# FFN down projection: the plain block moved from last to first, and the low parts of the other down weights made on VectorE instead of GpSimd

## The chip, the cores and the metric

The kernel runs on one core of a Trainium2 chip. The metric is the device time of one execution in microseconds (us); the times shown are medians of several runs.

## The reference

Two blocks on 1024 tokens of width 1024: first an RG-LRU with latent attention layer and an SSD layer, then a second block with gated convolution, stick-breaking attention, a feed-forward part and a gated per-layer embedding. The change concerns the end of the second block:

```
m = rmsnorm(h, g_mlp[i])
h = h + jnp.square(jax.nn.relu(m @ w_up[i])) @ w_down[i]
gate = jax.nn.sigmoid(rmsnorm(h, g_ple[i]) @ w_ple_gate[i])
h = h + gate * (p[i] @ w_ple_proj[i])
return rmsnorm(h, g_final)
```

`w_up` is 1024 x 4096 and `w_down` is 4096 x 1024.

## The kernel before

**Number format.** TensorE multiplies float32 values of reduced precision. Each operand is split into a high part and a low part (the value minus its high part), and each product is three matmuls: weight high with activation high, weight high with activation low, weight low with activation high. The high part of a weight is made by ScalarE (`down_hi`) or GpSimd (`plain_slab`), the low part by GpSimd (`down_part` at L946, `plain_slab` at L920). The parts live in `w_hi` and `w_lo`, a ring of eight entries of 128x256; an entry comes free when TensorE has finished the product that read it.

**Seven products.** The up and down projections are mostly computed as a two by two block product with seven instead of eight products (`SEVEN = [1, 6, 5, 7, 2, 3, 4]`). That needs sums and differences of weight quarters (`weight_sums`, four instructions of 128x256 on VectorE, L3448 to L3453) and of activations (`diff`, L3416, in `ffn_whole_u`). VectorE adds each product from PSUM into `H` or into `ffn_shared`, the part that three quadrants of the result have in common (`down_added`, L3477 and L3479). After all blocks `shared_added` (L3489) adds `ffn_shared` to the three quadrants of `H`.

**Order of work.** The hidden width 4096 is eight blocks of 512 (`FFN_BLOCKS`). The up projection runs over 16 pairs of slabs and stores its squared results to DRAM (`f_kept`). The down projection takes a block at a time, with the 512 x 1024 weights of a block in four slabs; a slab is seven products of six matmuls. Blocks 0 to 6 are done with seven products, block 7 (`last_down`, L1742) plainly, with 48 matmuls a slab. Then the gate's eight slabs follow (L991, `N_PLE`), which need the finished `H` in high and low parts (`raw_hi` on ScalarE, `raw_lo` on VectorE) and its squares (`raw_square`, `raw_add`).

**Queues.** Each engine works through an order written out by hand. On VectorE, a slab of the down projection is: wait for product i, add it; after the first add the four weight sums of the next slab; after some adds one step for the u tiles of the next block (`next_u_steps`: four differences in the second slab, four low parts in the third, three in the fourth, none in the first; L3416 and L3422). On ScalarE it is the seven high parts of the next slab (L2482), with the high parts of the next block's u (L2439) between them. GpSimd only makes low parts of weights there. SP issues all loads and stores: the next block's u tiles when the block before it is done, and each weight slab when the slab that held its place has been split.

**Waits of a product.** Product i on TensorE (`down`, L1720) waits for its weight's low part. In the first slab of a block it also waits for the low part of u. The fifth, sixth and seventh product of a slab share a PSUM bank with the first, third and fourth, and wait until VectorE has added those (`BEFORE = {2: 1, 3: 5, 4: 7}`); the first four wait for adds of the slab two earlier. The up pairs have the same scheme; the sixth product of the last pair waits for `c22` (L3367). In the last pair's VectorE order, two differences and a low part of block 0's u (`diff(5, 0)`, `u_lo(1, 0)`, `diff(6, 0)`) stand ahead of `u3` and `c22`.

Of the kernel before, what the change touches and what calls it, by code (L numbers as in the profile page):

```python
# [197 lines left out]
FFN_ORDER += [("down", _b, _s) for _b in range(DOWN_BLOCKS) for _s in range(4)]  # L198
FFN_ORDER += [("last", FFN_BLOCKS - 1, _s) for _s in range(4)]
# [27 lines left out]
for _n in range(pair_slab(PAIRS), N_PLE - 4):  # L227
    _uses(_n, 7, {6: _n + 1}, 1)
LAST_FREED = _freed
USED += USED[-1:] * (-len(USED) % RING)  # L230
for _n in range(N_PLE - 4, NSLAB):
    ENTRY[_n] = len(USED)
    USED += [("slab", _n + 1)] * 4
assert all(ENTRY[_n] % 4 == 0 for _n in range(N_PLE - 4, NSLAB))
DOWN_ADDS = 28 * DOWN_BLOCKS
# [18 lines left out]
HIGHS = [(_j, _b) for _b in range(FFN_BLOCKS) for _j in ((1, 5, 6, 7, 2, 3, 4) if _b < DOWN_BLOCKS else (1, 8, 2, 3))]  # L254
LOWS = [(_j, _b) for _b in range(FFN_BLOCKS) for _j in (SEVEN if _b < DOWN_BLOCKS else (1, 8, 2, 3))]
DIFFS = [(_j, _b) for _b in range(DOWN_BLOCKS) for _j in (5, 6, 7, 4)]
# [40 lines left out]
def product_turn(b, s, j):  # L297
    return 7 * (4 * b + s) + SEVEN.index(j) + 1
# [23 lines left out]
def program(nc, x_t, pos, w, vec, rows, consts, p_t, out):  # L322
    ctx = ExitStack()
    with ctx:
# [146 lines left out]
        def head_square_at(k):  # L471
# [25 lines left out]
        u_even_at = {1: raw_at, 4: raw_at + 8 * kb, 5: xh_at + 48 * kb, 3: xh_at + 56 * kb, 6: xh_at, 2: xh_at + 8 * kb, 7: xh_at + 16 * kb}  # L497
        u_odd_at = {1: raw_at + 16 * kb, 6: raw_at + 24 * kb, 5: raw_at + 32 * kb, 7: raw_at + 40 * kb,
                    2: xh_at + 32 * kb, 3: xh_at + 40 * kb, 4: xh_at + 24 * kb}
        u_plain_at = {8: xh_at + 24 * kb, 1: xh_at + 32 * kb, 2: xh_at + 40 * kb, 3: xh_at + 48 * kb}  # L500
        u_at = {"even": u_even_at, "odd": u_odd_at, "plain": u_plain_at, "later": {5: raw_at + 48 * kb}}
        U_SPLIT = {(name, j): place(at_, f"ffn_u_{name}{j}", [P, 2, 2, HB], F32R)[0] for name, table in u_at.items() for j, at_ in table.items()}
        U_WHOLE = {(name, j): place(at_, f"ffn_whole_u_{name}{j}", [P, 2, 2, HB], F32)[0] for name, table in u_at.items() for j, at_ in table.items()}
        PJ = (place(xh_at, "ple_proj_a", [P, 6, TOK], F32)[0], place(xh_at + 56 * kb, "ple_proj_b", [P, 2, TOK], F32)[0])
# [21 lines left out]
        def u_name(b, j):  # L526
            if b == DOWN_BLOCKS:
                return "plain", j
            if b % 2:
                return "odd", j  # L530
            return "later" if j == 5 and b else "even", j
# [105 lines left out]
        s_hk = sem("h_kept_then_ffn_plain_u_loaded")  # L637
# [41 lines left out]
        s_u7 = Part(s_hk, 16 * KT)  # L679
# [59 lines left out]
        def _(sp):  # L739
# [38 lines left out]
            def load(b, j):  # L778
                t, half = 0 if j in (1, 8) else 1, 0 if j in (1, 2) else HB
                to = 4 if j == 8 and b < DOWN_BLOCKS else j  # L780
                done = s_u7 if b == DOWN_BLOCKS else s_ur[b % 2][RAW_QUAD[j]]
                sp.dma_start(u_whole(b, to),
                             f_kept[2 * b:2 * b + 2, t, :, half:half + HB].rearrange("q p t -> p q t")).then_inc(done.sem, 16)

            d0 = pair_slab(PAIRS)
# [11 lines left out]
            next_slab(d0)  # L797
            next_slab(d0 + 1)
# [6 lines left out]
            used(pair_use(p, 1))  # L805
            load(0, 3)
            used(pair_use(p, 2))
            load(0, 2)
            store(p, 0)
            store(p, 1)  # L810
            for b in range(DOWN_BLOCKS):
                if b == 0:
                    used(pair_use(p, 6))
                    stored(4)
                else:
                    sp.wait_ge(s_slab, FFN_AT["down", b - 1, 3] + 1)
                    stored(2 * b + 4)
                for j in (1, 8, 3, 2):
                    load(b + 1, j)
                for s in range(2, 6):  # L820
                    next_slab(d0 + 4 * b + s)
            for n in range(d0 + 4 * DOWN_BLOCKS + 2, NSLAB):
# [12 lines left out]
        def _(pool):  # L835
# [112 lines left out]
            d0 = pair_slab(PAIRS)
# [21 lines left out]
        class Down:  # L970


            def wait(self, eng, k):
                eng.wait_ge(s_dr, DOWN_ADDS + k + 1)

        @block.tensor
        def _(pe):
# [747 lines left out]
            def last_down(q):  # L1725
# [2042 lines left out]
```

## Time and profile before

| | us |
|---|---|
| median of 3 runs | 2628.53 |
| lowest, highest | 2624.53, 2628.74 |
| the profiled execution | 2624.4 |
| its span | 2622.5 |
| TensorE busy | 2542.3 (97%) |
| VectorE busy | 1730.9 (66%) |
| ScalarE busy | 1147.0 (44%) |
| GpSimd busy | 1136.2 (43%) |

Busy times are of the profiled execution, whose own time is 2624.4 us. In the profile PE is TensorE, PEld its weight loads, DVE VectorE, ACT ScalarE, POOL GpSimd and SP SyncE. A busy time is a union over instructions, whose recorded durations overlap: from the start of one instruction to the start of the next is less than the duration.

### The profile page before, as it was taken

The page shows a single profiled execution, that of the slowest core. Times are in us where ns is not written, and L with a number is a line of the kernel's source. Part 1 is how long each engine was busy: PE and PEld are TensorE (multiplying, and loading weights), DVE is VectorE, ACT ScalarE, POOL GpSimd, SP SyncE. Part 2 cuts the span into 40 slices and gives each one's busy share as a digit, 9 for nine tenths or more (in the row PEclk, how much of TensorE's full clock was granted, in tenths as well). Part 3 has the DMA queues.
Part 4 walks back from the last instruction along what each step waited for, and adds up shares of the span by engine and source line. Part 5 has one row for each costly group of instructions (what it writes and reads, how often), then busy time and mean ns, then how long its engine had stood idle before and what let it go on. Part 6 is the DMA issues. An engine that isn't in the chain of part 4 may idle for free.

```text
span 2622.5 us, 33254 instructions
## 1 busy us (share of the span) xinstructions
PE 2542.3 (97%) x12712; PEld 2022.7 (77%) x12712; DVE 1730.9 (66%) x2061; ACT 1147.0 (44%) x1757; POOL 1136.2 (43%) x1100
## 2 busy tenths in 40 slices
PE   8999999999999999999999999999999998999997
PEld 7877888687787787887676777767888887878886
DVE  7636763677748648658776455565556668999856
ACT  3527882336405305316275545463333334444232
POOL 4633344532342432432441222214645556777652
PEclk9999999999999999999999999999999999999999
DMA  3111002212212112111230001002133333322412
GB/s 140 49 44 33 25 25 86 92 47 101 65 49 81 57 48 73 64 49 61 84 129 25 33 25 33 25 25 97 49 126 107 113 113 121 121 98 104 161 41 81
DMA packets 58137, 189.93 MB, mean 72 GB/s; under 512 B 5952, under 2 KB 6336, under 8 KB 57984
## 3 DMA queue, kind: packets, MB, share of 16 engines
q1 hardware_dynamic: 44704, 143.67, 16.1%
q10 hardware_dynamic: 13280, 44.17, 4.7%
q8 instruction: 102, 1.67, 0.3%
q14 instruction: 51, 0.42, 0.1%
HBM read 158.33 MB, written 29.49 MB: 72 GB/s over the span
## 4 chain that ended last, share of the span: by engine, by line
PE 80%; DVE 11%; ACT 5%; issue 3%; POOL 1%; ACTq 0%; DMA 0%; DVEq 0%; POOLq 0%; SPq 0%
PE PS L991 38%; PE PS L1697 10%; PE PS L1720 8%; PE PS L1321 4%; PE PS L1228 3%; PE PS L1742 2%; PE PS L1554 1%; PE PS L1537 1%; PE PS L1354 1%; PE PS L1127 1%; PE PS L1364 1%; PE PS L1358 1%; PE PS L1141 1%; PE PS L1577 1%; PE PS L1670 1%
## 5 line engine op out<-in xcount | busy, mean ns | idle before, releaser
L839 POOL CAST w_hi<-w_stage 128x1024 fp32r<-128x1024 f32 x130 | 144.4, 1111 | 1046.9 <-PE PS L991 756.9
L842 POOL TENSOR_TENSOR w_lo<-w_stage,w_hi 128x256 fp32r<-128x256 f32 x520 | 494.0, 981 | 10.4
L991 PE MATMUL PS<-XH,w_hi 128*128 128x512 f32 x1216 | 386.6, 399 | 9.0 <-ACT ssd_z L2136 3.3
L991 PE MATMUL PS<-XL,w_hi 128*128 128x512 f32 x1216 | 375.5, 390 | 0.0
L991 PE MATMUL PS<-XH,w_lo 128*128 128x512 f32 x1216 | 375.0, 390 | 0.0
L991 PEld LDWEIGHTS PS<-XH,w_hi 128*128 128x128 f32 x1216 | 221.4, 188 | 65.5 <-issue 12.9
L991 PEld LDWEIGHTS PS<-XL,w_hi 128*128 128x128 f32 x1216 | 228.2, 188 | 48.8
L991 PEld LDWEIGHTS PS<-XH,w_lo 128*128 128x128 f32 x1216 | 228.2, 188 | 48.6
L946 POOL TENSOR_TENSOR w_lo<-w_sums,w_hi 128x256 fp32r<-128x256 f32 x112 | 126.1, 1138 | 59.7 <-ACT w_hi L2482 59.1
L1697 PE MATMUL PS<-ffn_token_sums,w_hi 128*128 128x512 f32 x448 | 138.0, 389 | 0.0
L1720 PE MATMUL PS<-ffn_u_even,w_hi 128*128 128x512 f32 x400 | 125.6, 395 | 5.3 <-DVE ffn_shared L3477 3.2
L934 POOL TENSOR_TENSOR w_lo<-up_w_sums,w_hi 128x512 fp32r<-128x512 f32 x56 | 82.7, 1478 | 80.7 <-ACT w_hi L2470 80.5
L2096 ACT ACTIVATE ssd_x<-ssd_conv 128x1024 f32<-128x1024 f32 x16 | 16.9, 1060 | 227.2 <-DVE ssd_conv L2924 222.5
L1697 PE MATMUL PS<-ffn_raw,w_hi 128*128 128x512 f32 x336 | 104.7, 393 | 2.3 <-DVE ffn_t L3367 2.3
L1720 PE MATMUL PS<-ffn_u_odd,w_hi 128*128 128x512 f32 x336 | 104.3, 392 | 1.1 <-DVE H L3479 0.4
L3479 DVE TENSOR_TENSOR H<-H,PS 128x512 f32<-128x512 f32 x140 | 93.4, 679 | 17.0 <-PE PS L1720 15.5
L1697 PEld LDWEIGHTS PS<-ffn_token_sums,w_hi 128*128 128x128 f32 x448 | 84.1, 188 | 17.4
L1720 PEld LDWEIGHTS PS<-ffn_u_even,w_hi 128*128 128x128 f32 x400 | 74.8, 190 | 25.4 <-issue 7.7
L2924 DVE SCALAR_TENSOR_TENSOR ssd_conv<-PS,VC,ssd_conv 128x1023 f32<-128x1023 f32 (+2 forms) x72 | 92.3, 1282 | 2.6
L2922 DVE TENSOR_SCALAR ssd_conv<-PS,VC 128x1024 f32<-128x1024 f32 x24 | 32.2, 1343 | 92.6 <-PE PS L991 92.5
L3240 DVE TENSOR_TENSOR sb_z<-sb_z,PS 128x1024 f32<-128x1024 f32 (+3 forms) x48 | 45.8, 954 | 67.3 <-PE PS L1554 67.0
L946 POOL TENSOR_TENSOR w_lo<-w_stage,w_hi 128x256 fp32r<-128x256 f32 x84 | 82.5, 990 | 15.3 <-ACT w_hi L2482 15.3
(492 smaller groups left out, 6105.1 us busy)
## 6 DMA issues: line engine op xcount, KB each, us to landing
w_stage<-w SPq DMA_DIRECT2D x202, 512.0 KB, 3.3
ssd_sum_rows<-sums_kept ACTq DMA_DIRECT2D x32, 512.0 KB, 3.8
f_kept<-ffn_t SPq DMA_DIRECT2D x32, 512.0 KB, 2.6
ffn_whole_u_even<-f_kept SPq DMA_DIRECT2D x16, 512.0 KB, 4.8
ffn_whole_u_odd<-f_kept SPq DMA_DIRECT2D x12, 512.0 KB, 5.4
H<-x_t ACTq DMA_DIRECT2D x8, 512.0 KB, 8.2
pj_kept<-ple_proj_tiles ACTq DMA_DIRECT2D x8, 512.0 KB, 2.6
h_kept<-H ACTq DMA_DIRECT2D x8, 512.0 KB, 3.6
```

Source lines behind the costliest of these rows:

```text
L839: nc.gpsimd.tensor_copy(w_hi[:, slot, :, :], w_stage[:, slot, :, :]).then_inc(s_w_hi, 1)
L842: nc.gpsimd.tensor_tensor(w_lo[:, slot, k:k + 2, :], w_stage[:, slot, k:k + 2, :], w_hi[:, slot, k:k + 2, :].bitcast(F32), ALU.subtract).t ...
L934: nc.gpsimd.tensor_tensor(ring(w_lo, e, 2), src, ring(w_hi, e, 2).bitcast(F32), ALU.subtract).then_inc(done, count)
L946: nc.gpsimd.tensor_tensor(ring(w_lo, e), src, ring(w_hi, e).bitcast(F32), ALU.subtract).then_inc(done, count)
L991: mm = nc.tensor.matmul(outs[:, half, :], wt[:, slot, k, :], a[:, k - first, half * HB:(half + 1) * HB], start=(k == whole[0] and wt is w_ ...
L1228: mm = nc.tensor.matmul(PS[:, 2 * (n % 2) + half, :], wt[:, n % 2, k, :], a[:, k, half_cols(half)], start=(k == 0 and wt is w_hi and a is ...
L1321: mm = nc.tensor.matmul(PS[:, half, :], wt[:, n % 2, k, :], a[:, k, half * HB:(half + 1) * HB], start=(k == 0 and wt is w_hi and a is XH), ...
L1697: mm = nc.tensor.matmul(PS[:, 4 * (p % 2) + BANK[j], :], ring(wt, e + 2 * i + k // 2, k % 2), up_acts(j, hl, k), start=(j not in BEFORE an ...
L1720: mm = nc.tensor.matmul(PS[:, 4 * (d % 2) + BANK[j], :], ring(wt, e + i, k), down_acts(b, j, k, hl), start=(j not in BEFORE and k == 0 and ...
L1742: mm = nc.tensor.matmul(PS[:, 4 * (q % 2) + 2 * e + half, :], ring(wt, e0 + k // 2, k % 2), down_acts(DOWN_BLOCKS, quad, t % 2, hl), start ...
L2924: ins = v.scalar_tensor_tensor(out=y[:, d:TOK], in0=src[:, 0:TOK - d], scalar=wcol(3 - d), in1=y[:, d:TOK], op0=ALU.mult, op1=ALU.add)
L3479: v.tensor_tensor(dst, dst, src, ALU.add).then_inc(s_dr, 1)
```

## The change

- The plain block is block 0 and comes first (`plain_down`); blocks 1 to 7 follow with seven products. The numbers of matmuls stay the same.
- VectorE makes the low parts of the weights of the 28 slabs with seven products (`down_lo`), seven a slab, one ahead of each add. GpSimd keeps the plain slabs.
- The last pair's VectorE order has `u_lo(1, 0)` and `u_lo(8, 0)` ahead of `u3`, and `u_lo(2, 0)`, `u_lo(3, 0)` behind it. Differences and low parts of block 1's u are made beside the plain block.
- The shared sums are added inside the last block, after the second add of each slab. `last_tile` (raw_lo and the square's add) also stands inside the last block, and so do ScalarE's `gate_acts`.
- The u tiles have other places in memory. The loads of `pj_kept` are issued by SP instead of ScalarE.

```diff
-FFN_ORDER += [("down", _b, _s) for _b in range(DOWN_BLOCKS) for _s in range(4)]
-FFN_ORDER += [("last", FFN_BLOCKS - 1, _s) for _s in range(4)]
+FFN_ORDER += [("plain", 0, _s) for _s in range(4)]
+FFN_ORDER += [("down", _b, _s) for _b in range(1, FFN_BLOCKS) for _s in range(4)]
...
-            for d in range(4 * DOWN_BLOCKS):
-                for i in range(7):
-                    down_part(d, i)
-            for turn, n in enumerate(range(N_PLE - 4, NSLAB)):
-                plain_slab(n, 2 * PLAIN_PAIRS + turn)
+            for c in range(4):
+                plain_slab(PLAIN_DOWN + c, 2 * PLAIN_PAIRS + c)
+            pool.wait_ge(s_w_ready, 4 * N_PLE)
+            for c, n in enumerate(range(N_PLE, NSLAB)):
+                plain_slab(n, 2 * PLAIN_PAIRS + 4 + c)
...
+            def gate_acts(k):
                 Down().wait(act, k)
                 raw_hi(ple, "g_ple", k)
                 raw_square(ple, k)
+
+            for d in range(4 * DOWN_BLOCKS):
+                b = d // 4 + 1
+                highs = [j for j, b_ in HIGHS if b_ == b + 1]
+                for i in range(7):
+                    down_hi(d, i)
+                    if highs and d % 4 == 2 and i in (1, 3, 5):
+                        u_hi(highs[i // 2], b + 1)
+                    if highs and d % 4 == 3 and i in (1, 2, 4, 6):
+                        u_hi(highs[(1, 2, 4, 6).index(i) + 3], b + 1)
+                    if not highs and d % 4 and i == 5:
+                        gate_acts(2 * (d % 4 - 1))
+                    if not highs and d % 4 > 1 and i == 1:
+                        gate_acts(2 * (d % 4 - 1) - 1)
+            for k in range(5, KT):
+                gate_acts(k)
...
+            def down_lo(d, i):
+                n, j = SEVEN_DOWN + d, SEVEN[i]
+                e = ENTRY[n] + i
+                src = stage(n)[:, RAW_AT[j]:RAW_AT[j] + 2, :] if j in RAW_AT else WS[:, SUM_AT[j], :, :]
+                s_ah.wait(dve, 7 * (PAIRS - PLAIN_PAIRS) + 7 * d + i + 1)
+                done, count = (s_wd, 1) if i < 6 else (s_w_ready, 4)
+                v.tensor_tensor(ring(w_lo, e), src, ring(w_hi, e).bitcast(F32), ALU.subtract).then_inc(done, count)
...
+            def shared_added(s):
+                dve.wait_ge(s_dr, product_turn(FFN_BLOCKS - 1, s, 6))
+                for h in (H[:, 2 * s + 1, HB:TOK], H[:, 2 * s, HB:TOK], H[:, 2 * s + 1, 0:HB]):
+                    v.tensor_tensor(h, h, SHARED[:, s, :], ALU.add).then_inc(s_dv.sem, 1)
+
+            def down_added(b, s):
...
                 for i, j in enumerate(SEVEN):
+                    if ahead:
+                        down_lo(d + 1, i)
+                        if i == 0:
+                            weight_sums(*ahead)
...
+                    if end and i == 1:
+                        shared_added(s)
+                    if end and s and i == 2:
+                        last_tile(2 * s - 1)
+                    if end and i == 6:
+                        if s == 2:
+                            for slot in range(2):
+                                v.memset(SM[:, 4 + slot, 0:1], 0.0).then_inc(s_evac[slot], 4 * FFN_BLOCKS)
+                        last_tile(2 * s)
```

## Rows read from the trace of the kernel before

**Rows 1.** The page: busy line of the engines, and the chain's shares by engine.
```profile
PE 2542.3 (97%) x12712; PEld 2022.7 (77%) x12712; DVE 1730.9 (66%) x2061; ACT 1147.0 (44%) x1757; POOL 1136.2 (43%) x1100
...
PE 80%; DVE 11%; ACT 5%; issue 3%; POOL 1%; ACTq 0%; DMA 0%; DVEq 0%; POOLq 0%; SPq 0%
```
**Rows 2.** Windows: us, then busy (x) of PE, PEld, DVE, ACT, POOL; clock, DMA, GB/s.
```profile
2191.70:2274.40 82.70, 77.34 (x326) 61.01 (x324) 77.38 (x114) 38.15 (x75) 59.58 (x56) 0.98 0.33 115
...
2313.50:2352.90 39.40, 39.06 (x168) 31.21 (x169) 36.55 (x56) 17.19 (x36) 29.73 (x29) 1.00 0.32 108
2352.90:2392.00 39.10, 38.86 (x168) 31.27 (x168) 36.28 (x55) 17.23 (x36) 29.71 (x29) 1.00 0.30 108
```
**Rows 3.** The chain that ended last: start, us, what; end of the down projection.
```profile
2431.19 41.06 PE PS L1720 x180
2472.26 43.52 PE PS L1742 x192
```
**Rows 4.** Timelines of TensorE and VectorE, 2178 to 2204: start, us, instruction, idle before.
```profile
2184.53 0.70 PE L1697 MATMUL PS<-ffn_raw,w_hi 128*128 128x512 f32 x2 [2.31 <-DVE ffn_t L3367]
...
2196.13 0.70 PE L1720 MATMUL PS<-ffn_u_even,w_hi 128*128 128x512 f32 x2 [0.85 <-DVE ffn_u_even L3422]
2196.67 0.39 PE L1720 MATMUL PS<-ffn_u_even,w_lo 128*128 128x512 f32 x1
...
2202.35 1.19 PE L1720 MATMUL PS<-ffn_u_even,w_hi 128*128 128x512 f32 x2 [3.25 <-DVE ffn_shared L3477]
2203.34 0.63 PE L1720 MATMUL PS<-ffn_u_even,w_lo 128*128 128x512 f32 x1
...
2178.56 2.21 DVE L3422 TENSOR_TENSOR ffn_u_even<-ffn_whole_u_even,ffn_u_even 128x1024 fp32r<-128x1024 f32 x1
2180.69 2.31 DVE L3416 TENSOR_TENSOR ffn_whole_u_even<-ffn_whole_u_even,ffn_whole_u_even 128x1024 f32<-128x1024 f32 x1
```
**Rows 5.** Timeline of VectorE in one slab with four steps.
```profile
2338.54 0.46 DVE L3448 TENSOR_TENSOR w_sums<-w_stage 128x256 f32<-128x256 f32 x1
...
2339.37 0.42 DVE L3451 TENSOR_TENSOR w_sums<-w_stage 128x256 f32<-128x256 f32 x1
2339.71 0.42 DVE L3453 TENSOR_TENSOR w_sums<-w_stage,w_sums 128x256 f32<-128x256 f32 x1
2340.05 0.68 DVE L3479 TENSOR_TENSOR ffn_shared<-ffn_shared,PS 128x512 f32<-128x512 f32 x1
2340.64 1.23 DVE L3422 TENSOR_TENSOR ffn_u_even<-ffn_whole_u_even,ffn_u_even 128x1024 fp32r<-128x1024 f32 x1
2341.79 0.67 DVE L3479 TENSOR_TENSOR H<-H,PS 128x512 f32<-128x512 f32 x1
...
2348.83 0.46 DVE L3448 TENSOR_TENSOR w_sums<-w_stage 128x256 f32<-128x256 f32 x1
```
**Rows 6.** Groups of instructions, 2274 to 2430: busy us, mean ns, then idle before.
```profile
L946 POOL TENSOR_TENSOR w_lo<-w_sums,w_hi 128x256 fp32r<-128x256 f32 x65 | 75.1, 1167 | 31.2 <-ACT w_hi L2482 30.8
...
L2482 ACT ACTIVATE w_hi<-w_sums 128x256 fp32r<-128x256 f32 x64 | 24.3, 409 | 57.2 <-DVE w_sums L3450 49.3 <-PE PS L1720 7.5
...
L3422 DVE TENSOR_TENSOR ffn_u_even<-ffn_whole_u_even,ffn_u_even 128x1024 fp32r<-128x1024 f32 x12 | 15.8, 1316 | 0.0
```
**Rows 7.** Groups of VectorE, ScalarE (2472 to 2530) and GpSimd (2472 to 2600).
```profile
L3276 DVE SCALAR_TENSOR_TENSOR raw_lo<-H,VC,raw_hi 128x1024 fp32r<-128x1024 f32 x8 | 11.5, 1439 | 0.0
L3489 DVE TENSOR_TENSOR H<-H,ffn_shared 128x512 f32<-128x512 f32 x12 | 8.4, 770 | 0.0
...
L2394 ACT ACTIVATE raw_hi<-H,VC 128x1024 fp32r<-128x1024 f32 x8 | 9.2, 1151 | 39.3 <-DVE H L3495 30.6 <-DVE H L3499 8.7
L2403 ACT ACTIVATE ffn_t<-H 128x1024 f32<-128x1024 f32 x8 | 8.4, 1046 | 1.2 <-DVE square_sum L3285 1.2
...
L920 POOL TENSOR_TENSOR w_lo<-w_stage,w_hi 128x256 fp32r<-128x256 f32 x43 | 42.3, 995 | 0.0
L909 POOL CAST w_hi<-w_stage 128x256 fp32r<-128x256 f32 x42 | 25.8, 629 | 52.0 <-PE PS L991 29.1 <-PE PS L1742 22.9
```

More of the change, by code:

```diff
@@ L526, in u_name, with u_loaded @@
         def u_name(b, j):
-            if b == DOWN_BLOCKS:
+            if b == 0:
                 return "plain", j
-            if b % 2:
-                return "odd", j
-            return "later" if j == 5 and b else "even", j
+            if b == 1 and j == 4:
+                return "first", j
+            return ("even", "odd")[b % 2], j
+        def u_loaded(b):
+            return 16 * (b // 2 + 1)
         def down_acts(b, j, i, hl):
@@ L805, in _ @@
             used(pair_use(p, 1))
+            load(0, 2)
             load(0, 3)
-            used(pair_use(p, 2))
-            load(0, 2)
             store(p, 0)
@@ L2434, in u_hi @@
                 if j in RAW_QUAD:
-                    done, count = (s_u7, 64) if b == DOWN_BLOCKS else (s_ur[b % 2][RAW_QUAD[j]], 16 * (b // 2 + 1))
-                    done.wait(act, count)
+                    s_ur[b % 2][RAW_QUAD[j]].wait(act, u_loaded(b))
                 else:
@@ L3462, in next_u_steps @@
                 return {1: (u_lo, 2), 3: (u_lo, 3), 5: (u_lo, 4)}
-            def down_added(b, s, ahead, steps):
-                n, d = FFN_AT["down", b, s], 4 * b + s
+            def shared_added(s):
[3 more added lines that the diff above has]
+            def down_added(b, s):
+                n, d, end = FFN_AT["down", b, s], 4 * (b - 1) + s, b == FFN_BLOCKS - 1
+                ahead = None if end and s == 3 else (b, s + 1) if s < 3 else (b + 1, 0)
+                steps = next_u_steps(b + 1, s) if s and not end else {}
                 into = {1: SHARED[:, s, :], 6: SHARED[:, s, :], 5: H[:, 2 * s + 1, HB:TOK], 7: H[:, 2 * s + 1, HB:TOK],
@@ L3475, in down_added @@
                         dve.wait_ge(s_dr, product_turn(b, s, 1 if j == 6 else 5))
-                    if j == 1 and b == 0:
+                    if end and j in (5, 3, 4):
+                        s_dv.wait(dve, 3 * s + {5: 1, 3: 2, 4: 3}[j])
+                    if j == 1 and b == 1:
                         v.tensor_copy(dst, src).then_inc(s_dr, 1)
@@ L3527, in _ @@
                 f(3, p)
+                if last:
+                    u_lo(2, 0)
                 f(1, p)
                 if last:
-                    weight_sums(0, 0)
-                    diff(7, 0)
-                    diff(4, 0)
+                    u_lo(3, 0)
                 c12(p)
                 f(8, p)
-                if last:
-                    u_lo(6, 0)
                 c21(p)
                 f(2, p)
-            for j in (5, 7, 2, 3, 4):
-                u_lo(j, 0)
-            for d in range(4 * DOWN_BLOCKS):
-                steps = {}
-                if d % 4:
-                    steps = next_u_steps(d // 4 + 1, d % 4)
-                down_added(d // 4, d % 4, ((d + 1) // 4, (d + 1) % 4) if d + 1 < 4 * DOWN_BLOCKS else None, steps)
-            for s in range(4):
-                shared_added(s)
-            for q in range(4):
-                last_even(q)
-                if q == 2:
-                    v.memset(SM[:, 4, 0:1], 0.0).then_inc(s_evac[0], 4 * FFN_BLOCKS)
-                if q:
-                    last_tile(2 * q - 1)
-                last_odd(q)
-                if q == 2:
-                    v.memset(SM[:, 5, 0:1], 0.0).then_inc(s_evac[1], 4 * FFN_BLOCKS)
-                last_tile(2 * q)
+            diff(5, 1)
+            diff(6, 1)
+            plain_even(0)
+            diff(7, 1)
+            diff(4, 1)
+            u_lo(1, 1)
+            plain_odd(0)
+            u_lo(6, 1)
+            u_lo(5, 1)
+            plain_even(1)
+            u_lo(7, 1)
+            u_lo(2, 1)
+            plain_odd(1)
+            u_lo(3, 1)
+            weight_sums(1, 0)
+            plain_even(2)
+            down_lo(0, 0)
+            down_lo(0, 1)
+            u_lo(4, 1)
+            plain_odd(2)
+            down_lo(0, 2)
+            down_lo(0, 3)
+            plain_even(3)
+            down_lo(0, 4)
+            down_lo(0, 5)
+            plain_odd(3)
+            down_lo(0, 6)
+            for b in range(1, FFN_BLOCKS):
+                for s in range(4):
+                    down_added(b, s)
             last_tile(KT - 1)
```

198 lines of the change are left out of this document (74 added, 124 removed).

## The prediction

> **What bounds the kernel now.** I read the page's busy line and its chain first. TensorE is busy 97% of the span and holds 80% of the chain, VectorE 11% [rows 1]. So a change can pay only where TensorE stands still, and it costs where another engine becomes slower than TensorE. VectorE's 66% is an average, so I cut the down projection into blocks of four slabs (28 products, 168 matmuls) with the windows view [rows 2]. A block takes 39.1 to 39.4 us, and in it VectorE is busy 36.3 to 36.6 us against GpSimd's 29.7. VectorE is at 93% there; that is the view that decides this case. TensorE's own need comes from the pieces of the chain [rows 3]: 180 matmuls in 41.06 us are 0.228 us each, so 38.3 us a block; the 192 matmuls of the plain slabs take 43.52 us.
>
> TensorE's stalls that the change touches are at the front [rows 4]: 2.31 us in the last up pair behind VectorE's L3367, then 0.85 and 3.25 us in the first down slab. After the longest one the same matmuls take 0.63 instead of 0.39 us for a while, and the granted clock of that stretch is 0.98 instead of 1.00 [rows 2, 4].
>
> **What one VectorE instruction costs.** Durations overlap, so I take start to start from a full slab [rows 5]. The four weight sums run from 2338.54 to 2340.05: 1.51 us, the independent one 0.34 us (2339.37 to 2339.71). One add of a product takes 0.60 us (2340.05 to 2340.64, rounded up), one step on a whole u tile (a low part; a difference has the same shape) 1.15 us (2340.64 to 2341.79). A slab with four steps is 7 x 0.60 + 4 x 1.15 + 1.51 = 10.3 us, and the rows run from 2338.54 to 2348.83, 10.29 us. The four slabs of a block carry 0, 4, 4 and 3 steps: 5.7, 10.3, 10.3 and 9.15, together 35.5 us.
>
> **Part 1: low parts of the weights on VectorE.** Each slab gets 7 tensor_tensor of 128x256 (down_lo), 28 a block. VectorE's own row of that shape, two SBUF inputs, is the weight sum: 0.34 us start to start, 0.42 us if the next one waits for it [rows 5]. Nothing behind down_lo on VectorE reads its result, so I take 0.34; below nothing it cannot fall by itself, only by what GpSimd's silence gives the other instructions (below). Per block that is 28 x 0.34 = 9.5 us, and VectorE needs 35.5 + 9.5 = 45.0 us where TensorE needs 38.3 and took 39.2. Both are chained. A slab's fifth to seventh product wait for VectorE's adds in the same slab, so TensorE runs at most some three products (4 us) ahead, and down_lo and adds are one queue, so VectorE's free time in the first slab (8.1 us of work) is used up by what it is behind. So the block costs 45.0. Blocks 1 to 6 carry steps for the block after them: 6 x (45.0 - 39.2) = +35 us.
>
> What comes back: GpSimd's 28 instructions a block no longer wait for ScalarE (1.17 us mean [rows 6]), but TensorE was not late behind them. With GpSimd silent the u low parts may fall from 1.32 us mean [rows 6] to the 1.21 to 1.23 of most rows in [rows 5]: 7 x 0.1 and little else, under 1 us a block. I take none of it in the sum and keep 6 us for the low end. The case for more is in the instruction at 2178.56, which took 2.21 us beside a GpSimd instruction [rows 4]. The Trainium skill (SBUF — State Buffer, the section on the shared port pair) says that a VectorE instruction with two SBUF inputs and a GpSimd instruction lock each other out for a whole instruction. This trace agrees for that row, but in full blocks VectorE's mean is only 0.1 us above its usual one; by the rule at its fullest each of the 11 steps and 16 sums could gain up to one GpSimd instruction, and the change would pay.
>
> Waits added: down_lo waits for ScalarE's high part, which waits for the product before it in the slab on TensorE. In its queue stand all adds behind it. In blocks 1 to 6 VectorE is behind TensorE, and ScalarE (0.41 us each [rows 6], 17 us busy a block) has made the part long before; cost nothing, and at worst one ScalarE copy, 0.4 us, for each of the 7 first slabs.
>
> **Part 2: the plain block first.** TensorE's matmuls are the same, 192 + 1176. VectorE's work ahead of the last pair's c22 falls from two differences and one low part to two low parts (1.15 each), and they wait for two loads instead of three. TensorE got c22's result at 2184.53 and wanted it at 2182.2; without the 2.31 us instruction, and with the 2.21 us one at its usual 1.2, it is there at about 2181.2. I count the stall of 2.31 us and the slow matmuls behind it (1.8 us, 9 at 0.2 more each) as gone: the pairs end at 2187.6 instead of 2191.7. The plain slabs then need only two, later four, low parts of u, made by then, and run 43.5 us without a stall, to 2231.1. Beside them VectorE has 4 differences, 7 u low parts, 8 adds of 128x1024 (1.2 each), 4 sums and 7 down_lo: 13 + 10 + 1.5 + 2.4 = 27 us, hidden in 43.5, and its f_kept loads arrive long before the first wait. GpSimd's plain slabs cost 4 x (0.63 + 1.0) = 6.5 us [rows 7] beside 10.9 us of TensorE. The first down slab starts with everything ready, and its 4.1 us of stalls are gone too.
>
> **Part 3: the last block.** It has no u steps, but gains 12 shared adds (0.6 start to start each, 0.77 in the rows; formerly beside the plain slabs) and the gate's eight last_tile, raw_lo and square add, of the steps' shape, at some 1.15 each (raw_lo's row is 1.44 beside GpSimd) [rows 7]. Also ScalarE does raw_hi (1.15) and the square (1.05) of an even tile before the high part that the seventh down_lo waits for: in three slabs VectorE stands 1.15 + 1.05 + 0.4 = 2.5 us, since that starts only after the sixth add. Slab 0: 4.2 + 2.4 + 1.5 + 1.8 + 1.1 + 2.5 = 13.5; slabs 1 and 2: 4.2 + 2.4 + 1.5 + 1.8 + 4.6 + 2.5 = 17 each; in slab 3 TensorE waits for the fourth add: 4 x 0.6 + 1.8 + 2.3 = 6.5, then its last product 1.4. Together 55 us.
>
> **The sum, in the profiled execution.** From 2231.1: the first block 47.4 (1.7 + 8.1 held to TensorE's pace, 0.6 lag, then 36.9), five blocks of 45.0, the last 55.4: 327.8, so the gate's matmuls start at 2558.9. They start at 2515.78 now [rows 3]; behind them nothing changes. +43.1. TensorE now stands 1.6 us at a time before the sixth product, in the last block 2 to 3 us, and stalls of 2.3 and 3.25 us were the ones with slow matmuls behind them [rows 4]: +2 us for one or two such stretches on the path. 2624.4 + 45 = 2669.5. The median of runs, 2628.5, is 4 above that execution and its lowest, 2624.5, level with it: I say 2670.
>
> **Rivals.**
> 1. VectorE has room (faster). If a down_lo costs at most (39.2 - 35.5) / 28 = 0.13 us net of what GpSimd's silence returns, TensorE still sets the pace, only the front's gain stays, 4.1 in the last pair, 4.1 of stalls and 1.8 of slow matmuls in the first slab: 2628.5 - 10 = 2618. It decides at 0.13 us; the nearest row has 0.34 [rows 5]. 5%.
> 2. TensorE's clock. If the stalls in each slab pull the granted clock to the lower level for most of a slab, 42 matmuls take 42 x (0.228 + 0.2) = 18 us (0.2: 0.63 less 0.39 in the rows, rounded down, about double the spacing and so the level of half speed) against VectorE's 12.7, +5 on 18 slabs: 2628.5 + 43 + 18 x 5 = 2760; one short spell a slab hides in the 3 us that TensorE waits. For it: two stalls over 2 us did it; against it: the 0.85 us stall did not [rows 4]. The Trainium skill (TensorE: Matmul & The Clock Gate, Part 1) has idle time lower the clock to half, and the trace shows that level. 8%.
> 3. down_lo costs 0.42 us, or in-order waits for ScalarE stand in every slab: 196 x 0.08 = +16: 2686. 15%.
> 4. ScalarE's turn in the last block and the lag at the first are hidden: 2670 - 7.5 - 2 - 6 (GpSimd's silence) = 2655. 20%; the forecast itself has the other 52%.
>
> **Numbers.** The range goes from 2648 (rival 4 with down_lo at 0.30, below every row: 196 x 0.04 = 8 us less) to 2700 (rival 3 with the clock's spells in the last block not hidden, some 14 us). This kernel's measurement tells 0.2%, 5 us. Faster 0.05, same 0.02, slower 0.93.
>
> **What would show it.** Blocks 1 to 6 of 45 us with VectorE busy throughout and TensorE's waits named after VectorE's adds (ffn_shared, H) instead of nothing; VectorE's new instruction near 0.42 us; no stall at L3367's place; the plain slabs still 43.5 us; the last block some 55 us. Wrong: blocks near 39 us, or waits of VectorE for ScalarE's w_hi as the longest of its list, or a clock well below 1.00 in blocks 1 to 6.

## The result, and the profile after

The changed kernel takes 2673.31 us (median of 4 runs, 2671.0 to 2674.89), the kernel before 2626.6 (4 runs on the same chip): a ratio of 1.0176 (95% interval 1.0161 to 1.0190), or +47 us. The forecast was 2670. The profiled execution took 2671.0 us, its span 2668.9. Two single executions of the experiments, 5742.86 us in experiment 1 and 7796.53 us of the kernel before beside it, lie far above all others and count in no ratio.

The page after, where [rows 1] stood before. TensorE has the same 12712 matmuls; VectorE has 196 instructions more and GpSimd 196 fewer, and VectorE's share of the chain has risen from 11% to 16%:

```profile
PE 2551.6 (96%) x12712; PEld 2019.9 (76%) x12712; DVE 1785.6 (67%) x2257; ACT 1147.2 (43%) x1757; POOL 931.6 (35%) x904
...
PE 73%; DVE 16%; ACT 5%; issue 4%; DMA 1%; POOL 1%; ACTq 0%; SPq 0%; DVEq 0%; POOLq 0%
```

The windows of after, with the columns of [rows 2]: the plain slabs, the first block of seven products, two in the middle, then the last block.

```profile
2187.20:2230.50 43.30, 43.30 (x192) 35.87 (x191) 29.33 (x30) 10.02 (x14) 20.05 (x24) 1.00 0.33 122
2230.50:2276.30 45.80, 40.05 (x170) 31.00 (x169) 43.18 (x81) 17.48 (x36) 0.00 (x0) 1.00 0.31 115
2276.30:2321.10 44.80, 40.11 (x169) 30.80 (x168) 44.40 (x83) 17.18 (x35) 0.00 (x0) 1.00 0.27 95
2321.10:2365.90 44.80, 40.21 (x170) 30.96 (x170) 44.54 (x85) 17.25 (x35) 0.00 (x0) 1.00 0.27 94
...
2499.90:2562.70 62.80, 46.21 (x170) 34.25 (x169) 53.34 (x90) 20.16 (x34) 10.57 (x13) 0.89 0.26 92
```

In a middle block VectorE is busy 44.5 of 44.8 us, where it was busy 36.3 of 39.1 [rows 2]. TensorE's busy time has gone up by 1 us only. So the block is as long as VectorE's queue. The chain of waits has these two pieces, to be laid beside [rows 3]: the plain slabs take 43.53 us at their new place against 43.52 at the old one, and the gate's matmuls start at 2562.66 instead of 2515.78, +46.9 us.

```profile
2187.16 43.53 PE PS L1735 x192
...
2562.66 7.48 PE PS L984 x33
```

What TensorE waits for in the seven blocks (2230.5 to 2562.7): us in total, times, longest. Every entry is VectorE's add, L3477 or L3479:

```profile
PE PS L1713 <- DVE H L3479: 35.2, 37, 2.8
PE PS L1713 <- DVE ffn_shared L3479: 9.0, 13, 3.1
PE PS L1713 <- DVE ffn_shared L3477: 0.8, 2, 0.4
```

VectorE's timeline of a slab with four steps, which answers to [rows 5]. A low part takes 0.33 us start to start (2347.26 to 2347.59, 2349.33 to 2349.66), an add 0.60, a low part of u 1.14 (2348.19 to 2349.33). The slab is 12.54 us (2346.66 to 2359.20) instead of 10.29:

```profile
2346.66 0.68 DVE L3479 TENSOR_TENSOR ffn_shared<-ffn_shared,PS 128x512 f32<-128x512 f32 x1
2347.26 0.42 DVE L3442 TENSOR_TENSOR w_lo<-w_sums,w_hi 128x256 fp32r<-128x256 f32 x1
2347.59 0.68 DVE L3479 TENSOR_TENSOR ffn_shared<-ffn_shared,PS 128x512 f32<-128x512 f32 x1
2348.19 1.22 DVE L3400 TENSOR_TENSOR ffn_u_even<-ffn_whole_u_even,ffn_u_even 128x1024 fp32r<-128x1024 f32 x1
2349.33 0.42 DVE L3442 TENSOR_TENSOR w_lo<-w_sums,w_hi 128x256 fp32r<-128x256 f32 x1
2349.66 0.68 DVE L3479 TENSOR_TENSOR H<-H,PS 128x512 f32<-128x512 f32 x1
...
2359.20 0.68 DVE L3479 TENSOR_TENSOR ffn_shared<-ffn_shared,PS 128x512 f32<-128x512 f32 x1
```

The last block by slabs (same columns): 19.4, 17.2, 16.1 and 10.1 us. The first of these windows begins 4.7 us ahead of the slab's first add.

```profile
2499.90:2519.30 19.40, 17.09 (x67) 13.11 (x65) 15.87 (x32) 5.48 (x12) 0.00 (x0) 0.91 0.17 55
2519.30:2536.50 17.20, 10.34 (x42) 7.65 (x42) 14.59 (x26) 6.32 (x12) 0.00 (x0) 1.00 0.09 30
2536.50:2552.60 16.10, 13.87 (x42) 9.97 (x42) 13.53 (x24) 7.79 (x11) 3.43 (x4) 0.69 0.12 35
2552.60:2562.70 10.10, 4.91 (x19) 3.52 (x20) 9.35 (x12) 0.58 (x1) 7.15 (x10) 1.00 0.93 361
```

### The profile page after: what moved, and what is told of

It is laid out like the page before. It is cut to its first block, busy times and chain, and to the rows that moved or that the text cites. A ratio compares the mean times of both kernels' runs of the same rounds, so it can differ in the third digit from the quotient of the medians.

```text
span 2668.9 us, 33211 instructions
## 1 busy us (share of the span) xinstructions
PE 2551.6 (96%) x12712; PEld 2019.9 (76%) x12712; DVE 1785.6 (67%) x2257; ACT 1147.2 (43%) x1757; POOL 931.6 (35%) x904
## 3 DMA queue, kind: packets, MB, share of 16 engines
q1 hardware_dynamic: 45760, 147.87, 16.1%
## 4 chain that ended last, share of the span: by engine, by line
PE 73%; DVE 16%; ACT 5%; issue 4%; DMA 1%; POOL 1%; ACTq 0%; SPq 0%; DVEq 0%; POOLq 0%
PE PS L984 37%; PE PS L1690 10%; PE PS L1314 4%; PE PS L1221 2%; PE PS L1713 2%; DVE H L3479 2%; PE PS L1735 2%; DVE w_lo L3442 1%; PE PS L1547 1%; PE PS L1530 1%; PE PS L1347 1%; PE PS L1120 1%; DMA w_stage<-w 1%; PE PS L1357 1%; PE PS L1351 1%
## 5 line engine op out<-in xcount | busy, mean ns | idle before, releaser
L848 POOL TENSOR_TENSOR w_lo<-w_stage,w_hi 128x256 fp32r<-128x256 f32 x520 | 491.8, 976 | 10.4
L915 POOL CAST w_hi<-w_stage 128x256 fp32r<-128x256 f32 x64 | 46.5, 740 | 391.3 <-DVE w_lo L3442 332.3
L1713 PE MATMUL PS<-ffn_u_odd,w_hi 128*128 128x512 f32 x432 | 139.8, 406 | 30.5 <-DVE H L3479 23.1
L1713 PEld LDWEIGHTS PS<-ffn_u_odd,w_hi 128*128 128x128 f32 x432 | 80.8, 193 | 59.0 <-issue 23.3
L1713 PE MATMUL PS<-ffn_u_even,w_hi 128*128 128x512 f32 x336 | 105.7, 396 | 13.7 <-DVE H L3479 11.3
L3479 DVE TENSOR_TENSOR H<-H,PS 128x512 f32<-128x512 f32 x140 | 94.8, 678 | 2.3 <-PE PS L1713 1.8
L2474 ACT ACTIVATE w_hi<-w_sums 128x256 fp32r<-128x256 f32 x112 | 43.1, 409 | 115.3 <-DVE w_sums L3428 61.6
```

Of the source, the lines that this page charges most:

```text
L848: nc.gpsimd.tensor_tensor(w_lo[:, slot, k:k + 2, :], w_stage[:, slot, k:k + 2, :], w_hi[:, slot, k:k + 2, :].bitcast(F32), ALU.subtract).t ...
L915: nc.gpsimd.tensor_copy(ring(w_hi, e), src).then_inc(s_eh.sem, 1)
L1713: mm = nc.tensor.matmul(PS[:, 4 * (d % 2) + BANK[j], :], ring(wt, e + i, k), down_acts(b, j, k, hl), start=(j not in BEFORE and k == 0 and ...
L3479: v.tensor_tensor(dst, dst, src, ALU.add).then_inc(s_dr, 1)
```

## The experiments

The numbers are those of the names under which they ran; there is no 6. Ratios are against the kernel before, on the same chip, with 95% intervals.

**1 to 3. How many low parts VectorE makes.** After, with GpSimd's `down_part` restored: VectorE makes none, two or four of a slab's seven.

```diff
+ON_DVE = ()            # (1, 4) and (0, 1, 3, 5) in the other two
...
                     if ahead:
-                        down_lo(d + 1, i)
+                        if i in ON_DVE:
+                            down_lo(d + 1, i)
```

> The changed kernel with all low parts of the weights back on GpSimd; plain block first and the last block's order stay. Theory (VectorE's time alone sets the blocks, 35.5 us of its old work plus 0.335 us a low part, against TensorE's 39.2): blocks 1 to 6 fall from 44.7 to 39.2 us, the front's gain of 10 us stays, the last block stays bound by VectorE at some 44 us: 2621 us, 5 less than the kernel before. Rival A (the new order itself, memory places or the plain block first, costs most of the 47 us): 2650 or more. Rival B (the front's gain is taken back elsewhere): 2627 or more.

> As the kernel with all low parts on GpSimd, but two of seven (i = 1 and 4) on VectorE, 8 a block. Theory: 35.5 + 8 x 0.335 = 38.2 us of VectorE, under TensorE's 39.2, so the blocks stay at 39.3 and only the last block pays some 2 us: 2623. Rival C (each low part costs by its wait in VectorE's queue and not by VectorE's sum, so the cost is linear in their number): 2/7 of the whole cost of 50 us, 2635.

> Four of seven low parts (i = 0, 1, 3, 5) on VectorE, 16 a block, three on GpSimd. Theory: 35.5 + 16 x 0.335 = 40.9 us a block, plus up to 0.8 of contention with GpSimd, against 39.2: six blocks cost 10 to 15 us, the last one some 5: 2638. Rival C (linear): 2621 + 4/7 of 50 = 2650.

Measured: none 2646.55 (ratio 1.0069, 1.0048 to 1.0091; 2645.4 without the execution of 5742.86 us), two 2651.35 (1.0094, 1.0076 to 1.0112), four 2667.49 (1.0157, 1.0139 to 1.0176). One middle block of each, in that order, one kernel to a fence:

```profile
2321.40:2361.70 40.30, 39.11 (x169) 31.19 (x169) 37.85 (x56) 17.42 (x36) 28.38 (x28) 1.00 0.29 106
```
```profile
2320.30:2362.30 42.00, 39.27 (x170) 31.15 (x169) 40.46 (x64) 17.40 (x36) 19.67 (x20) 1.00 0.29 100
```
```profile
2327.80:2371.90 44.10, 39.95 (x170) 31.01 (x169) 43.30 (x73) 17.28 (x36) 8.97 (x12) 1.00 0.29 98
```

Block times are 40.3, 42.0, 44.1 and 44.8 us for 0, 8, 16 and 28 low parts on VectorE. That they are the cause is shown. In this order of work the first few aren't free either: the first eight cost 0.21 us each, the next eight 0.26, the last twelve, with which GpSimd falls silent, 0.06. But all four kernels have the weight sums ahead of the first add, and that alone brings a block from 39.2 to 40.3 us (experiment 5), so none of them starts with room on VectorE. Whether a few low parts would be free with the sums behind the add was not run. My arithmetic for the rest of the change fell with the first run: I had expected 2621 without the low parts and got 2646, and experiments 2 and 3 missed with it (2623 and 2638 expected). Over the first they cost 6 and 22 us, where I had 2 and 17. The other edits, which I had down as a gain, cost 18 us. Experiments 5, 7, 10 and 12 look for those.

**4. ScalarE's turn in the last block.** After, with the even tiles' `gate_acts` behind the seventh high part instead of ahead of it:

```diff
-                    if not highs and d % 4 and i == 5:
+                    if not highs and d % 4 and i == 6:
                         gate_acts(2 * (d % 4 - 1))
```

> The changed kernel, in which ScalarE does raw_hi and the square of tiles 0, 2 and 4 behind the seventh high part of the slab instead of ahead of it. Theory (VectorE stands 2.5 us in each of three slabs of the last block, waiting for that high part): the three waits go, 7.5 us, and with the longest stalls some of the time at TensorE's lower clock: 2665. Rival D (the wait is hidden by what VectorE does next, or TensorE's lower clock sets the last block): 2672 or more.

Measured 2666.67 (1.0153, 1.0135 to 1.0172), 6.6 us below the change. VectorE's waits in the last block, of after and then of this kernel:

```profile
DVE w_lo L3442 <- ACT w_hi L2474: 7.6, 3, 2.5
DVE H L3479 <- PE PS L1713: 1.5, 2, 0.9
```
```profile
DVE H L3479 <- PE PS L1713: 2.1, 3, 0.8
DVE raw_lo L3263 <- ACT raw_hi L2387: 0.6, 2, 0.3
```

Three waits of 2.5 us, 7.6 in all, are gone. The median falls by 6.6 and the profiled execution by 7.0 (2671.0 to 2664.01): in-order waits on the queue that sets the pace cost nearly their whole length.

**5. Sums behind the add.** Experiment 1's kernel had its weight sums ahead of the slab's first add, where the kernel before has them behind.

```diff
-                        if i == 0:
-                            weight_sums(*ahead)
...
                         v.tensor_tensor(dst, dst, src, ALU.add).then_inc(s_dr, 1)
+                    if i == 0 and ahead:
+                        weight_sums(*ahead)
```

> As the kernel with all low parts on GpSimd (2646.5), but the four weight sums stand behind the first add again, as in the kernel before, and not ahead of it. Theory (there the blocks took 40.35 us and not 39.2, since the second add then waits for the first one's result, 0.72 instead of 0.60 us start to start, and the first u step collides with a GpSimd instruction on two SBUF inputs, 1.69 instead of 1.21 us): blocks of 39.2 again, 6 x 1.15 = 7 us less: 2640. Rival E (memory places or loads of the new layout slow the blocks): 2645 or more.

Measured 2635.66 (1.0031, 1.0019 to 1.0044), about 10 us less than experiment 1 and 4 less than I expected. The middle block is back at 39.2 us with VectorE at 36.3, 1.2 us less in each of six blocks. In experiment 1 more of VectorE's instructions with two SBUF inputs were slow beside GpSimd's: a difference of u took 1.34 us on average, here 1.23, and the first sum 0.56, here 0.47. The last block, from TensorE's first matmul in it to the gate's, takes 55.8 us (59.7 in experiment 1) and is not at a block's pace:

```profile
2313.80:2353.00 39.20, 38.89 (x170) 31.34 (x169) 36.34 (x56) 17.24 (x35) 29.76 (x29) 1.00 0.31 107
...
2468.80:2524.60 55.80, 44.74 (x170) 34.43 (x169) 49.84 (x68) 19.77 (x34) 35.30 (x36) 0.91 0.25 90
```

**7. Squares out of the last block.** Experiment 5's kernel, with `raw_lo` alone in the last block and squares and their adds behind it.

```diff
                    if end and s and i == 2:
-                        last_tile(2 * s - 1)
+                        raw_lo(ple, "g_ple", 2 * s - 1)
```

> As the last one, and in the last block ScalarE makes only raw_hi and VectorE only raw_lo; the eight squares and their seven adds follow behind the last slab, beside the gate's first slab. Theory (the last block takes 58 us instead of 39 because VectorE has the squares' adds in it and ScalarE's squares hold back high parts of weights, both while TensorE waits): VectorE has 16.8 + 4.5 + 7.2 + 7 x 1.15 = 36.6 us in it, under TensorE's 38.3, so the block takes 40 to 42 us and the kernel 2617 to 2622, below the kernel before. Rival F (raw_hi alone still holds back ScalarE, or the square sum comes too late for the gate): 2630 or more.

A miss: 2633.28 (10 runs; 1.0024, 1.0014 to 1.0033). The last block fell from 55.8 to 49.4 us and not further. I put that down to the shared adds, which still stood ahead of the third add; experiment 10 moves them, but `raw_lo` with them, so which of the two it was isn't shown. And the squares, now late, made the gate wait:

```profile
2534.11 1.28 PE L1293 MATMUL PS<-square_sum,CN 128*128 128x512 f32 x2 [3.78 <-DVE square_sum L3298]
```

**8. The low parts alone.** The kernel before, with VectorE making 189 of the 196 low parts and nothing else changed.

```diff
-            for d in range(4 * DOWN_BLOCKS):
-                for i in range(7):
-                    down_part(d, i)
+            for i in range(7):
+                down_part(0, i)
...
                 for i, j in enumerate(SEVEN):
+                    if ahead:
+                        down_lo(d + 1, i)
```

> The kernel before with one part of the change alone: VectorE makes the low parts of the weights of all slabs with seven products but the first (189 of 196). Theory: blocks 0 to 5 need 35.5 + 28 x 0.335 = 44.9 us of VectorE, less the first slab's seven, against 39.2; block 6 has fewer steps and stays under TensorE: 6 x 5.6 - 2 = +32 us: 2659. Rival G (low parts on VectorE cost only together with the plain block's new place): 2635 or less.

Measured 2662.59 (1.0134, 1.0117 to 1.0151): +35 us by the ratio, 37.5 by the two medians. A stretch as long as a block of it, 45 us with VectorE at 44.5, and TensorE's longest wait in it:

```profile
2300.00:2345.00 45.00, 40.88 (x169) 32.34 (x168) 44.49 (x84) 17.01 (x35) 0.00 (x0) 0.96 0.26 93
...
2320.99 1.19 PE L1721 MATMUL PS<-ffn_u_even,w_hi 128*128 128x512 f32 x2 [2.04 <-DVE H L3495]
```

The granted clock is 0.96 here, not 1.00: TensorE waits 2.03 to 2.06 us once or twice a block, and behind some of these waits a few matmuls run at the lower level (1.19 us for two instead of 0.70). VectorE still sets the block, 45.0 to 45.9 us, so these spells are nearly hidden.

**9. What GpSimd's silence is worth.** After, with 168 differences of 128x256 on GpSimd in blocks 1 to 6, on constants, each released by the same high part as the low part on VectorE. Nothing waits for them.

```diff
+            for d in range(4 * (DOWN_BLOCKS - 1)):
+                for i in range(7):
+                    s_ah.wait(pool, 7 * (PAIRS - PLAIN_PAIRS) + 7 * d + i + 1)
+                    nc.gpsimd.tensor_tensor(spare, const[:, 0:256], const[:, 256:512], ALU.subtract).then_inc(s_spare, 1)
```

> The changed kernel, with 168 differences of 128x256 on GpSimd in blocks 1 to 6, one behind each high part of a weight, on constants and into a spare place; nobody waits for them. Theory (GpSimd's silence gives VectorE about 1 us a block back): 6 x 0.5 to 1.5 us more, 2676 to 2682. Rival H (each VectorE instruction with two SBUF inputs waits for a whole GpSimd instruction whenever they meet, 0.5 us for some 20 of the 55 in a block): 60 us more, 2733. Rival I (no contention): 2673.

Measured 2707.35 (1.0308, 1.0291 to 1.0325): +34 us over the change, where I had expected 3 to 9 and the rival, the lock, 60. Five middle blocks take 49.9 to 51.2 us, 50.4 on average, 5.7 more than in the change. Groups of instructions in the middle blocks (busy us, mean ns, idle before), of after and then of this kernel:

```profile
L3479 DVE TENSOR_TENSOR H<-H,PS 128x512 f32<-128x512 f32 x101 | 68.5, 678 | 0.3
L3442 DVE TENSOR_TENSOR w_lo<-w_sums,w_hi 128x256 fp32r<-128x256 f32 x81 | 33.7, 416 | 0.0
L3442 DVE TENSOR_TENSOR w_lo<-w_stage,w_hi 128x256 fp32r<-128x256 f32 x60 | 24.9, 415 | 0.3 <-ACT w_hi L2474 0.2
```
```profile
L955 POOL TENSOR_TENSOR up_partial<-CN 128x256 f32<-128x256 f32 x132 | 120.7, 914 | 114.4 <-ACT w_hi L2482 109.8
L3487 DVE TENSOR_TENSOR H<-H,PS 128x512 f32<-128x512 f32 x100 | 67.6, 676 | 0.3 <-PE PS L1721 0.2
L3450 DVE TENSOR_TENSOR w_lo<-w_sums,w_hi 128x256 fp32r<-128x256 f32 x80 | 50.1, 626 | 0.0
L3450 DVE TENSOR_TENSOR w_lo<-w_stage,w_hi 128x256 fp32r<-128x256 f32 x60 | 30.3, 505 | 0.0
...
L3437 DVE TENSOR_TENSOR w_sums<-w_stage 128x256 f32<-128x256 f32 x20 | 8.4, 418 | 0.0
```

Two low parts of one slab, both recorded while GpSimd is at work:

```profile
2353.09 0.94 DVE L3450 TENSOR_TENSOR w_lo<-w_sums,w_hi 128x256 fp32r<-128x256 f32 x1
2357.17 0.41 DVE L3450 TENSOR_TENSOR w_lo<-w_stage,w_hi 128x256 fp32r<-128x256 f32 x1
```

The low parts, which read two SBUF tensors and are released by the same high part as GpSimd's instruction, go from 0.42 to 0.63 and 0.51 us on average. The adds, with one input in PSUM, stay at 0.68. The sums stay at 0.42; in the slab looked at they run while GpSimd waits for its next high part. This is what the Trainium skill says (SBUF — State Buffer, Terms and Who interferes with whom, on the shared port pair): the pair is locked for a whole instruction, and for VectorE that concerns an instruction with two SBUF inputs. This trace agrees in kind: the averages hide single low parts of 0.41 us and of 0.83 to 0.95 us. The longest are held some 0.5 us, less than the 0.74 us of GpSimd's shortest instruction.

**10 and 11. The last block put in order, without and with the low parts.** Experiment 7's kernel with the shared sums behind the seventh add, each slab's two `raw_lo` (and ScalarE's `raw_hi`) a slab later and two square adds beside the last slab; then the same last block in the changed kernel.

```diff
-                    if end and i == 1:
-                        shared_added(s)
-                    if end and s and i == 2:
-                        raw_lo(ple, "g_ple", 2 * s - 1)
+                    if end and s and i in (1, 3):
+                        raw_lo(ple, "g_ple", 2 * s - 2 + i // 2)
                     if end and i == 6:
+                        shared_added(s)
```

> Low parts on GpSimd, sums behind the first add, squares late (the kernel of 2633.3), and in the last block the shared sums are added behind the seventh add of a slab instead of behind the second, raw_lo of a slab's two tiles follows one slab later, and the first two square adds come beside the last slab. Theory (the shared adds delay the third add, for which the sixth product waits, 2 to 2.9 us a slab, and the squares' sum comes 4 us late for the gate): the last block takes 40 to 42 us instead of 47 and the 4.2 us stall behind the gate's first slab falls below 2: 2620 to 2624, level with or just below the kernel before at 2625. Rival F (VectorE's own work, stretched by GpSimd's locks, sets the last block and the sum): 2628 or more.

> The changed kernel, low parts on VectorE, with the same last block as the kernel beside it. Theory (in the changed kernel that block takes 60 us, of which VectorE's work without the squares and without waits for ScalarE is 16.8 + 4.5 + 7.2 + 7 + 21 x 0.335 = 42.5 us): 44 to 48 us, so 12 to 16 less than 2673.3: 2657 to 2661. If so, 2657 less the other one's time is what the low parts cost alone, 33 to 38 us: 6 x 5.5 and some 3 in the last block. Rival: the last block stays above 52 us, 2665 or more.

Measured 2627.99 (11 runs; 1.0002, 0.9993 to 1.0011) and 2663.70 (1.0144, 1.0129 to 1.0160). Both stand a little above what I expected. The last block is in order in each, 41.4 and 44.8 us instead of 62.8:

```profile
2472.10:2513.50 41.40, 38.78 (x169) 31.29 (x168) 38.85 (x59) 16.25 (x29) 29.55 (x36) 1.00 0.28 96
...
2530.30 2.07 PE L1293 MATMUL PS<-square_sum,CN 128*128 128x512 f32 x2 [4.98 <-DVE square_sum L3301]
```
```profile
2499.80:2544.60 44.80, 39.78 (x170) 30.94 (x169) 44.36 (x83) 16.37 (x29) 9.09 (x13) 1.00 0.26 93
```

The second kernel differs from the first in the low parts and in one thing more: its weight sums stand ahead of the first add, as in the change. The difference of both is 35.7 us. It agrees with experiment 8 (35 to 37.5), where the sums stand behind. What is left in the first of them is a 4.98 us stall for the gate's sum of squares.

**12. That stall moved.** Experiment 10's kernel with `square_total` in the middle of the gate's second slab, and `pj_kept`'s first load behind four weight slabs on SP's queue.

```diff
-                if k == 0:
-                    square_total(ple)
+                if k == 1:
+                    product(pair(n % 2), n, XH2, XL2, range(4), 0, range(8))
+                    square_total(ple)
+                    product(pair(n % 2), n, XH2, XL2, range(4, 8), 0, range(8)).then_inc(s_slab, 1)
```

> As the kernel with low parts on GpSimd and the relieved last block (2628.0), and TensorE sums the squares' partial sums after half of the gate's second slab instead of after its first, and the first load of pj_kept is issued behind four weight slabs instead of ahead of them. Theory (TensorE stood 5.4 us for that sum, and a weight slab landed 9.4 us after its issue in the first block): the 5.4 us stall and the 3.4 us at half clock behind it go, 1 to 2 us in the first block too: 2620 to 2623, below the kernel before at 2626. Rival (the root then comes too late for the gate's third slab, which needs the bank): 2626 or more.

Measured 2619.07 (11 runs, 2616.63 to 2621.88) against 2626.17 of the kernel before: 0.9974 (0.9965 to 0.9983). It is faster than both kernels, by 7 us than the one before. The last block:

```profile
2469.40:2510.90 41.50, 38.92 (x169) 31.30 (x168) 38.97 (x59) 16.27 (x29) 29.63 (x36) 1.00 0.28 97
```

The two edits of this kernel weren't tried apart, but they act at different places of the trace: the gate's stretch falls from 74.7 to 67.7 us (67.0 in the kernel before), and the first block, in which the load was moved, from 40.7 to 39.2.

## Why the prediction was right, and where it was off

**The whole +47 us, by runs.** The kernels make a chain from before to after by experiments 12, 10 and 11; its steps must add up, and what they tell is their sizes. Experiment 12 against the kernel before is the plain block first with everything else in good order: -7.1. In the traces that is 4.2 us less in the last pair, 6.9 less in the first block (46.1 to 39.2), and 2.4 more in the last one (39.1 to 41.5), which now has the gate's work in it. Experiment 11 against 10 is the low parts on VectorE, with the sums' place: +35.7. What is left is the last block's order, its hand-over to the gate and the load moved in experiment 12: 12 against 10 (8.9) and after against 11 (9.6), +18.5. The sum is 47.1.

**How near the forecast came.** 2670 was the sum for the profiled execution, 2669.5, kept for the median; the forecast's +45 stands against +46.6 between the profiled executions. Part of the nearness is luck: VectorE's queue came to the last block 0.7 us early and the gate's and later stretch took 0.5 us less, against 2.5 us that the last block took over the 55.4 and the 2 that the sum had for the clock.

- *VectorE's queue sets a block.* Right. 45.0 us predicted, 44.5 to 44.8 in the trace; a low part at 0.34, measured 0.33. VectorE is busy throughout, and TensorE's waits are named after the adds. Rival 1 needed at most 0.13 us per low part, at which a block stays at 39.2; the trace shows 0.33, and in experiment 8, with nothing else changed, 28 of them bring the block to 45.
- *The front.* Right. The pairs end at 2187.2 (predicted 2187.6), and the plain slabs take 43.5 us. Where the last pair's matmuls had waited 2.31 us [rows 4], TensorE's timeline of after has no wait, and 0.39 us for the single matmul, not 0.63. The agreement of the 2187.2 is in part luck: the last pair was 0.5 us ahead of the trace before by then, and in other kernels of the same code up to 4 us behind it. Counted from the same add of VectorE (L3356 before, L3343 after) the gain is 4.2 us:

```profile
2182.01 0.39 PE L1690 MATMUL PS<-ffn_raw,w_lo 128*128 128x512 f32 x1
```

- *The last block.* Mechanism right, size short. This is the term of the sum that was mis-sized. VectorE's queue comes to it at 2502.8 (predicted 2503.5) and the gate starts at 2562.66 (predicted 2558.9): 59.9 us for the 55.4 of the forecast. By slabs, counted as in the forecast from the low part and the sums that open VectorE's slab, it is 14.7, 17.2, 17.9 and 10.1 us, where I had 13.5, 17, 17 and 7.9. Most of the 4.5 us can be found in VectorE's timeline. In slab 0 it waits 0.88 us for TensorE's seventh product (at 2512.16). In the last two slabs GpSimd is at work again, for the gate's weights (its 3.43 and 7.15 us in the windows above), and VectorE's instructions with two SBUF inputs stretch: three shared adds take 3.04 us instead of 1.89, and a square add 1.76 instead of 1.22:

```profile
2506.25 1.89 DVE L3454 TENSOR_TENSOR H<-H,ffn_shared 128x512 f32<-128x512 f32 x3
...
2554.09 3.04 DVE L3454 TENSOR_TENSOR H<-H,ffn_shared 128x512 f32<-128x512 f32 x3
```

  With `raw_lo` (1.51 and 1.35 for 1.28) that is 2 us. The forecast had these instructions at 0.6 and 1.15 although the rows beside GpSimd had shown 0.77 and 1.44 [rows 7]: this is where the term was too small. TensorE waits up to 3.08 us in this block, and behind two of these waits two matmuls take 1.19 us, at the lower clock, instead of 0.70; the 0.88 us above is behind the first of them:

```profile
2509.22 1.19 PE L1713 MATMUL PS<-ffn_u_odd,w_hi 128*128 128x512 f32 x2 [2.18 <-DVE H L3479]
...
2537.37 1.19 PE L1713 MATMUL PS<-ffn_u_odd,w_hi 128*128 128x512 f32 x2 [3.08 <-DVE ffn_shared L3479]
```

- *ScalarE's turn.* Right: three waits of 2.54, 7.5 predicted, 6.6 to 7.0 measured by experiment 4. ScalarE's timeline shows the order, with the low part on VectorE behind it:

```profile
2512.88 1.15 ACT L2387 ACTIVATE raw_hi<-H,VC 128x1024 fp32r<-128x1024 f32 x1 [5.39 <-DVE H L3479]
2513.94 1.05 ACT L2396 ACTIVATE ffn_t<-H 128x1024 f32<-128x1024 f32 x1
2514.89 0.71 ACT L2474 ACTIVATE w_hi<-w_stage 128x256 fp32r<-128x256 f32 x2
...
2515.39 0.42 DVE L3442 TENSOR_TENSOR w_lo<-w_stage,w_hi 128x256 fp32r<-128x256 f32 x1 [2.54 <-ACT w_hi L2474]
```

- *The clock (rival 2).* It didn't happen in the change. Blocks 1 to 6 have a wait in each slab, up to 1.40 us, and stay at 1.00, the upper level. It was near: in experiment 8, with the sums behind the first add, waits reach 2.06 us and the clock of five blocks is 0.96. Even so a block took 45.0 to 45.9 us there, so spells of this size hide behind VectorE's queue, as the rival's own condition says:

```profile
2350.49 0.70 PE L1713 MATMUL PS<-ffn_u_odd,w_hi 128*128 128x512 f32 x2 [1.40 <-DVE H L3479]
```

- *GpSimd's silence.* Here the reasoning was off, though the sum was not. I wrote it down as under 1 us a block, and it is that for the u steps: their mean falls from 1.316 [rows 6] to 1.215. But it also stands behind the price of the low parts. With GpSimd working on the same release, 28 instructions a block cost VectorE 5.7 us a block (experiment 9: 50.4 against 44.7, the means of five blocks), and the low parts' own durations rise by 0.09 to 0.21. I took 0.34 from a weight sum, and sums stay at 0.42 recorded (0.34 start to start) even in experiment 9. The change makes GpSimd silent, so it was the right number for a reason that I hadn't given. The rule at its fullest, by which the change would pay, doesn't hold either: with GpSimd silent the u steps gained 0.1 us each and the sums, which were at 0.42 to 0.45 before, next to nothing, where it needed up to a whole GpSimd instruction each.
- *The rest of the change as a gain.* The forecast counted the front as -10 and didn't ask what the sums' new place costs, since VectorE had no slack anyway. With the low parts on GpSimd that place is 10 us (experiments 1 and 5). Within the change nothing of it shows: its blocks, sums ahead, take 44.6 to 44.9 us, and those of experiment 8, sums behind, 45.0 to 45.9. The change with the sums behind was not run.

- *Rivals 3 and 4.* A low part costs 0.33, not 0.42, and VectorE's waits for ScalarE's `w_hi` in blocks 2 to 6 are 0.2 us in all; nor was ScalarE's turn hidden. Neither came.

Open: the 1.5 us or so of the last block's 4.5 that neither the 0.88 nor the 2 us account for; and what the changed kernel would take with experiment 12's gate, which wasn't run. The runs put it near 2655 to 2657 (2663.7 less 7.0 to 8.9), an estimate.

## What to carry to other kernels

Before moving work to an engine, cut the stage into its repeating unit and add up that engine's queue there, start to start: an engine at 93% of a block has no room for 9.5 us of new work, whatever its 66% over the span says. In this kernel, once VectorE set the pace, its total work decided and the place of the sums didn't (blocks of 44.8 and 45 us), except that the waits in its queue were paid nearly in full; while it had 3 us of slack, the place of the same sums was worth 1.2 us a block. A reordering that loses by its passengers may win by itself: here the plain block first is worth 7 us once the low parts stay on GpSimd and the last block and the gate's sum are put in order.

## What the runs showed of the hardware

- VectorE's instructions with two SBUF inputs stretch beside GpSimd's (means of 0.42 to 0.51 and 0.63 us, 1.22 to 1.29 and 1.33; single ones of 0.42 to 0.94), those with an input in PSUM don't (0.68 both times). 168 GpSimd instructions of 0.91 us cost 34 us.
- In the change, waits of 0.4 to 1.4 us in each slab, for 270 us on end, left TensorE's clock at its upper level; behind waits of 2.18 and 3.08 us in the last block the next matmuls ran at the lower one (1.19 instead of 0.70 us for two). Behind waits of 2.17 us (at 2523.94) and 2.84 us (at 2557.88) they did not, while in experiment 8 they did behind one of 2.04 us and not behind others of 2.06, so the length of one wait doesn't tell it.
